# Attention in a hybrid encoder layer: query blocks run on over the heads, scores as two 64-row tiles, V turned in the projection banks

## What is computed

```
def _diff_attention(q, k, v, lam):
    # q, k: (B, 8 heads, 2 components, S, 64); v: (B, 8, S, 128)
    def block(qblk):                      # 128 queries
        s = einsum('bhcqd,bhckd->bhcqk', qblk, k) * scale
        p = softmax(s, axis=-1)
        a = p[:, :, 0] - lam * p[:, :, 1]
        return einsum('bhqk,bhke->bhqe', a, v)
    return lax.map(block, qb)
```

## Time and profile before

| | before |
|---|---|
| median of 3 runs | 1740.48 us (1738.78 to 1741.96) |
| profiled execution | 1740.36 us, span 1738.6 us |
| TensorE matmul busy | 1655.1 us, 95% |
| VectorE busy | 1037.4 us, 60% |
| ScalarE busy | 755.8 us, 43% |
| GpSimd busy | 771.0 us, 44% |
| chain that ended last | PE 60%, DVE 19%, ACT 10%, issue 10% |
| mean granted clock of TensorE | 0.990 |

### The profile page before, as it was taken

How to read it: one execution, slowest core, us unless ns; L and a number is a source line. 1 busy time by engine, 2 the same in 40 slices (tenths; PEclk the granted TensorE clock), 3 DMA queues, 4 the chain that set the end, 5 groups by cost and what they waited for, 6 DMA issues and landing times.

```text
span 1738.6 us, 24563 instructions
## 1 busy us (share of the span) xinstructions
PE 1655.1 (95%) x8235; PEld 1355.8 (78%) x8235; DVE 1037.4 (60%) x1692; ACT 755.8 (43%) x1462; POOL 771.0 (44%) x926
## 2 busy tenths in 40 slices
PE   4999999999999998999999999999999999999995
PEld 3788887887878877878787878787877788888784
DVE  6703676776676767787878787878776101235213
...
GB/s 169 13 134 30 31 49 73 24 51 70 24 60 61 25 86 61 37 61 40 57 41 55 42 54 45 52 45 51 48 61 49 254 128 259 169 74 95 121 72 97
DMA packets 137300, 129.08 MB, mean 74 GB/s; under 512 B 5089, under 2 KB 120354, under 8 KB 136226
## 3 DMA queue, kind: packets, MB, share of 16 engines
...
...
## 4 chain that ended last, share of the span: by engine, by line
PE 60%; DVE 19%; ACT 10%; issue 10%; DMA 1%; DVEq 1%; ACTq 0%; SPq 0%
PE ps L621 45%; PE ps L629 7%; DVE negmax L1351 2%; PE ps L803 2%; PE ps L811 2%; ACT probs L1794 2%; ACT aT_split L1799 2%; DVE aT_split L1356 1%; DMA v_f<-in_x 1%; DVE h_sum L1304 1%; DVE raw_b L1038 1%; DVE mix L1343 1%; DVE q_stack L1286 1%; DVE sigmoid_work L1038 1%; DVE h_sum L1234 1%
## 5 line engine op out<-in xcount | busy, mean ns | idle before, releaser
L621 PE MATMUL ps<-xn_split,w_split 128*128 128x512 f32 x4224 | 1032.9, 401 | 2.4 <-ACT v_f L1501 1.9
L621 PEld LDWEIGHTS ps<-xn_split,w_split 128*128 128x128 f32 x4224 | 789.5, 189 | 187.1 <-POOL w_split L560 2.3
L554 POOL TENSOR_TENSOR w_split<-w_raw,ones 128x256 fp32r<-128x256 f32 x416 | 318.8, 796 | 855.9 <-PE ps L621 812.8
L560 POOL TENSOR_TENSOR w_split<-w_raw,w_split 128x256 fp32r<-128x256 f32 x416 | 329.3, 822 | 8.2
L1794 ACT ACTIVATE probs<-ps,negmax 128x1024 f32<-128x1024 f32 x128 | 143.0, 1117 | 139.0 <-DVE negmax L1351 139.0
L621 PE MATMUL ps<-h_split,w_split 128*128 128x512 f32 x768 | 181.2, 396 | 0.1
L621 PEld LDWEIGHTS ps<-h_split,w_split 128*128 128x128 f32 x768 | 143.4, 188 | 35.1 <-issue 0.5
L1351 DVE TENSOR_REDUCE negmax<-ps 128x1 f32<-128x1024 f32 x128 | 150.2, 1214 | 4.5 <-PE ps L803 4.5
L1356 DVE TENSOR_TENSOR aT_split<-ps,aT_split 128x512 fp32r<-128x512 f32 x128 | 88.5, 691 | 90.5 <-ACT aT_split L1799 89.6
L803 PE MATMUL ps<-k_stack,q_stack 128*128 128x512 f32 x512 | 135.7, 407 | 7.0 <-DMA k_stack<-k_stack 7.0
L803 PEld LDWEIGHTS ps<-k_stack,q_stack 128*128 128x128 f32 x512 | 92.4, 191 | 25.7 <-DMA k_stack<-k_stack 5.4
...
## 6 DMA issues: line engine op xcount, KB each, us to landing
...
```

What stands on the lines that cost most here:

```text
L554: hi = pool.tensor_tensor(wsp[b][:, 0, ks_], raw[b][:, ks_], ones[:, 0:1].unsqueeze(2).to_broadcast([P, SPLIT_K, P]), ALU.mult)
L560: lo = pool.tensor_tensor(wsp[b][:, 1, ks_], raw[b][:, ks_], wsp[b][:, 0, ks_].bitcast(F32), ALU.subtract)
L621: mm = pe.matmul(ps[:, half, :], wsp[b][:, wl, k, :], moving[:, xl, k, cols], start=(k == 0 and n == 0), stop=(k == KT - 1 and n == 2))
```

## The change

- Scores: Q and K are stored as plain high and low parts, both components one over the other. A matmul contracts 64 rows: component 0 on rows 0 to 63, component 1 on rows 64 to 127, alternating, into different banks. Three passes by two halves by two components are twelve matmuls a block. Both components of the scores are ready together. The doubling DMAs go.
- K has two buffers, by the parity of the head. The loop over heads is unrolled by two. Scores of head h + 1, block 0, are issued in block 7 of head h, and so are its maxima, exponentials and mix. K and Q of the next head are split in blocks 5 and 6.
- The mix is two steps: the first product starts after the first exponential, ahead of the second low part. On ScalarE both high copies stand ahead of both exponentials.
- The filler: head 0 as before does one half ahead of its blocks; after that even blocks take 10 k-steps (8 in head 0) and odd blocks 6.
- V's transposes go to banks 1 and 0, in blocks 0 and 1 (head 0: ahead of the blocks and in block 0).
- ScalarE squares the output from PSUM, VectorE no longer does. The gate's clamp moves to VectorE's end of block 0, its three activations to ScalarE's end of block 0. The output's steps and the shuffles move by a block.

The diff, cut to its core (engine by engine: names, SyncE, TensorE, VectorE, ScalarE):

```diff
+def fills(first):
+    return (0, 8) + tuple(8 + 14 * (q // 2) + 8 + 6 * (q % 2) for q in range(ST)) if first else \
+        (0, 0) + tuple(16 * (q // 2) + 10 + 6 * (q % 2) for q in range(ST))
+def halves(first, q):
+    at = fills(first)
+    return [n for n in range(8) if at[q + 1] < 8 * (n + 1) <= at[q + 2]]
...
-        qs = sb("q_stack", [P, 2, S], F32R, at=a_scope)
-        ks = sb("k_stack", [P, 2, 2, S], F32R, at=a_scope)
+        qs = sb("aq_split", [P, 2, S], F32R, at=a_scope)
+        ks = [sb(f"ak_split{i}", [P, 2, S], F32R, at=a_scope) for i in range(2)]
...
-def double_keys(hh):
-    own = (slice(0, AD), slice(AD, P))
-    for c in range(2):
-        sp.wait_ge(a_qk_lo.sem, a_qk_lo.after(hh, c))
-        sp.dma_start(ks[own[1 - c], c].bitcast(F32), ks[own[c], c].bitcast(F32)).then_inc(k_doubled, 16)
...
-def a_scores(h, q):
+def a_scores(h, par, q):
     if q == 0:
-        pe.wait_ge(k_doubled, 32 * h + 32)
-        pe.wait_ge(a_qk_lo.sem, a_qk_lo.after(h, 3))
-    for c in range(2):
-        if q > 0:
-            pe.wait_ge(a_exp.sem, a_exp.after(h, 2 * (q - 1) + c))
-        elif not is_zero(h):
-            pe.wait_ge(a_exp.sem, a_exp.after(h, c) - 2)
-        for i in range(2):
-            for b in range(2):
-                mm = pe.matmul(ps[:, 2 + 2 * c + i, :], qs[:, c, q * P:(q + 1) * P],
-                               ks[:, c, b, i * HALF:(i + 1) * HALF], start=(b == 0), stop=(b == 1))
-        mm.then_inc(a_score.sem, 1)
+        pe.wait_ge(a_qk_lo.sem, a_qk_lo.after(h, 1))
+    if not (is_zero(h) and q == 0):
+        pe.wait_ge(a_exp.sem, a_exp.after(h, 2 * q - 1))
+    for i in range(2):
+        for n, (a, b) in enumerate(PASSES):
+            for c in range(2):
+                rows = slice(c * AD, (c + 1) * AD)
+                mm = pe.matmul(ps[:, 2 + 2 * c + i, :], qs[rows, a, q * P:(q + 1) * P],
+                               ks[par][rows, b, i * HALF:(i + 1) * HALF], start=(n == 0), stop=(n == 2))
+                if i == 1 and n == 2:
+                    mm.then_inc(a_score.sem, 1)
+def mix_round(h, q, i):
+    if i == 0:
+        pe.wait_ge(a_mix.sem, a_mix.after(h, 5 * q + 4))
+    if not (is_zero(h) and q == 0 and i == 0):
+        pe.wait_ge(a_tr_read.sem, a_tr_read.after(h, 2 * q + i - 1))
+    for n in range(4):
+        k = 4 * i + n
+        mm = pe.transpose(ps[:, 6, n * P:(n + 1) * P], am[q % 2][:, k * P:(k + 1) * P], ident[:])
     mm.then_inc(a_tr.sem, 1)
+def v_round(h, i, tile_half):
+    pe.wait_ge(proj_read, tile_half)
+    for n in range(4):
+        c = 4 * i + n
+        mm = pe.transpose(ps[:, 1 - i, n * P:(n + 1) * P], vz[:, 0, c * P:(c + 1) * P], ident[:])
+    mm.then_inc(a_vtr.sem, 1)
 def pv(h, n):
-    pe.wait_ge(a_tr_read.sem, a_tr_read.after(h, round_of(2 * n + 1, 1)))
-    if n > 0:
-        pe.wait_ge(a_rs.sem, a_rs.after(h, 2 * (n - 1)))
-    elif not is_zero(h):
-        pe.wait_ge(a_rs.sem, a_rs.after(h, 0) - 2)
+    pe.wait_ge(a_tr_read.sem, a_tr_read.after(h, 4 * n + 3))
+    if n == 0:
+        pe.wait_ge(a_vlo.sem, a_vlo.after(h, 1))
+    if not (is_zero(h) and n == 0):
+        pe.wait_ge(a_of.sem, a_of.after(h, 2 * n - 1))
     for k in range(KT):
         mm = product(ps[:, 7, 0:2 * P], lambda a: va[:, a, k, :], lambda b: at_s[:, b, k, :],
                      start=(k == 0), stop=(k == KT - 1))
...
 def squares(h, n):
-    pe.wait_ge(a_osq.sem, a_osq.after(h, n))
+    pe.wait_ge(a_of.sem, a_of.after(h, 2 * n + 1))
+    if not (is_zero(h) and n == 0):
+        pe.wait_ge(a_rs.sem, a_rs.after(h, 2 * (n - 1)))
     pe.matmul(ps[:, 7, 2 * P:4 * P], ones[:], osq[:], start=True, stop=True).then_inc(a_ss.sem, 1)
-def a_head(h, first, last):
...
-    a_scores(h, 0)
+def a_head(h, par, first, last):
+    at = fills(first)
+    base, per_head, hh = (G_GL, 0, 0) if last else (G_A, 4, h)
+    def filler(begin, end):
+        for n in range(8):
+            lo, hi = max(begin, 8 * n), min(end, 8 * n + 8)
+            if lo < hi:
+                if lo == 8 * n and n in (1, 2):
+                    pe.wait_ge(a_vlo.sem, a_vlo.after(h, n - 1))
+                proj_half(base, per_head, hh, n // 2, n % 2, begin=lo - 8 * n, end=hi - 8 * n)
+    read_by = 2 * (G_A + 4 * h)
     if first:
-        pe.wait_ge(proj_read, 2 * (G_M + 8 * (MH - 1) + 7) + 2)
-    v_round(0)
-    filler(0)
-    if not first:
-        squares(h - 1, 3)
+        a_scores(h, par, 0)
+        v_round(h, 0, read_by)
+        filler(0, at[1])
     for q in range(ST):
         mix_round(h, q, 0)
         if q + 1 < ST:
-            a_scores(h, q + 1)
-        else:
-            filler(7, begin=4, end=6)
+            a_scores(h, par, q + 1)
+        elif not last:
+            a_scores(h + 1, 1 - par, 0)
         mix_round(h, q, 1)
+        if q == 0 and not first:
+            v_round(h, 0, read_by)
+            squares(h - 1, 3)
+        if q == (0 if first else 1):
+            v_round(h, 1, read_by + 1)
         if q % 2 == 0 and q > 0:
             squares(h, q // 2 - 1)
-        if q < 5:
-            filler(q + 1, amid=(lambda: v_round(1)) if q == 0 else None)
-        elif q == 5:
-            filler(6, end=4)
-        elif q == 6:
-            filler(6, begin=4)
-            filler(7, end=4)
-        else:
-            filler(7, begin=6)
+        filler(at[q + 1], at[q + 2])
         if q % 2 == 1:
             pv(h, q // 2)
...
+def k_low(hh, par):
+    dve.wait_ge(a_qk_hi.sem, a_qk_hi.after(hh, 0))
+    dve.tensor_tensor(ks[par][:, 1], qkf[:, 1], ks[par][:, 0].bitcast(F32), ALU.subtract) \
+        .then_inc(a_qk_lo.sem, 1)
+def q_low(hh):
+    dve.wait_ge(a_qk_hi.sem, a_qk_hi.after(hh, 1))
+    dve.tensor_tensor(qs[:, 1], qkf[:, 0], qs[:, 0].bitcast(F32), ALU.subtract).then_inc(a_qk_lo.sem, 1)
...
+def mix_first(h, q):
+    b = q % 2
+    dve.wait_ge(a_exp.sem, a_exp.after(h, 2 * q))
+    dve.reciprocal(rden[:, 0, 0:1], den[:, b, 0:1]).then_inc(a_mix.sem, 1)
+    dve.wait_ge(a_mix.sem, a_mix.after(h, 5 * q))
+    dve.tensor_scalar(am[b][:], pr[:, 0], rden[:, 0, 0:1], None, ALU.mult).then_inc(a_mix.sem, 1)
+def mix_second(h, q):
+    b = q % 2
+    dve.wait_ge(a_exp.sem, a_exp.after(h, 2 * q + 1))
+    dve.reciprocal(rden[:, 0, 1:2], den[:, b, 1:2]).then_inc(a_mix.sem, 1)
+    dve.wait_ge(a_mix.sem, a_mix.after(h, 5 * q + 2))
+    dve.tensor_scalar(rden[:, 1, 0:1], rden[:, 0, 1:2], neglam[:], None, ALU.mult).then_inc(a_mix.sem, 1)
+    dve.wait_ge(a_mix.sem, a_mix.after(h, 5 * q + 3))
+    dve.scalar_tensor_tensor(am[b][:], pr[:, 1], rden[:, 1, 0:1], am[b][:], ALU.mult,
+                             ALU.add).then_inc(a_mix.sem, 1)
...
+def a_head(h, par, first, last):
+    if first:
+        maxima(h, 0)
+        mix_first(h, 0)
+        v_low_round(h, 0)
+        mix_second(h, 0)
     for q in range(ST):
+        a_low_round(h, q, 0)
+        nxt = (h, q + 1) if q + 1 < ST else None if last else (h + 1, 0)
+        if nxt is not None:
+            maxima(*nxt)
+            mix_first(*nxt)
+        a_low_round(h, q, 1)
+        if q == 0 and not first:
+            v_low_round(h, 0)
+        if q == (0 if first else 1):
+            v_low_round(h, 1)
+        if nxt is not None:
+            mix_second(*nxt)
         if q == 0:
+            dve.wait_ge(proj_read, 2 * (4 * h + G_A))
+            dve.tensor_scalar(aw[:], vz[:, 1], -1.0, LARGEST, ALU.mult, ALU.min).then_inc(a_gate_dve.sem, 1)
         if q == 1:
             if not first:
+                o_out_gate(h - 1, 3)
+                dve.wait_ge(a_ost.sem, a_ost.after(h - 1, 7))
             dve.wait_ge(a_gate_act.sem, a_gate_act.after(h, 2))
             dve.scalar_tensor_tensor(ga[:], vz[:, 1], again[:], aw[:], ALU.mult, ALU.mult) \
                 .then_inc(a_gate_dve.sem, 1)
+            if not first:
+                o_out_low(h - 1, 3)
+        if q in (2, 4) and not last:
+            shuffle(h + 1, q - 2)
+        if q in (3, 5, 7):
+            o_out_gate(h, q // 2 - 1)
+            o_out_low(h, q // 2 - 1)
+        if q == 5 and not last:
+            k_low(h + 1, 1 - par)
+        if q == 6 and not last:
+            q_low(h + 1)
...
+def exps(h, q):
     b = q % 2
+    for c in range(2):
+        if not (is_zero(h) and q == 0):
+            act.wait_ge(a_mix.sem, a_mix.after(h, 5 * q - 1))
         act.wait_ge(a_max.sem, a_max.after(h, 2 * q + c))
         act.activation(pr[:, c], ps[:, 2 + 2 * c:4 + 2 * c, :].rearrange("p b k -> p (b k)"), ACT.Exp,
                        bias=nmax[:, b, c:c + 1], accum_out=den[:, b, c:c + 1]).then_inc(a_exp.sem, 1)
+def v_high_round(h, i):
+    if i == 0 and not is_zero(h):
+        act.wait_ge(a_pv.sem, a_pv.after(h, -1))
+    act.wait_ge(a_vtr.sem, a_vtr.after(h, i))
+    act.activation(va[:, 0, 4 * i:4 * i + 4, :], ps[:, 1 - i, :].rearrange("p (k s) -> p k s", k=4),
+                   ACT.Copy).then_inc(a_vhi.sem, 1)
 def o_read(h, n):
     act.wait_ge(a_pv.sem, a_pv.after(h, n))
+    if not (is_zero(h) and n == 0):
         act.wait_ge(a_ost.sem, a_ost.after(h, 2 * (n - 1)))
```

(31 more changed lines are left out.)

226 lines of the change are left out of this document (53 added, 173 removed).

## The result

The changed kernel took 1751.61 us (median, 1749.46 to 1754.4), the kernel before 1740.03 beside it: ratio 1.0066, 95% interval 1.0048 to 1.0085. It is 11.6 us slower where 18 us less were forecast, and outside the forecast's range. The profiled execution took 1754.4, its span 1752.6. Two single executions that took far longer than the rest of theirs (8366.3 of the kernel before, beside the later runs, and 2028.2 of all_three) are left out of the ratios.

A forecast was written before the change was run, and what follows sets the result against it. TensorE was taken as the bound, but not alone: busy 582.16 of 603.96 us over seven heads. The last product ending 19.4 earlier, less 1.5 for the clock, gave 17.9 off 1740.36: 1722.4 us, range 1705 to 1748.

The forecast's parts named there:

- pair slot: Scores: two 64-row matmuls on both array halves run together in 0.237 us, so six pairs take 1.42.
- x: Time from a block's first four transposes to its second four; 2.05 forecast in q3, more where low parts come late.
- T: Moment when a block's first four transposes start on TensorE; other times in the block count from it, in us.
- dear switches: Rival: entering or leaving 64-row tiles costs 0.4 us, not 0.1; 17 lost in all, 1739, no change; chance 0.08.
- The start: Attention's opening: first scores at 656.0, first transposes of head 0 at 664.1 against 670.37 before.
- q0: First of a head's eight blocks, q0 to q7; forecast 10.5 us, second transposes 2.32 after the first.
- Block by block: Step walking through a steady head's eight blocks: sum 84.3 us a head against 86.28, 2.0 gained.
- q1: Block 1 of a head: new wait behind the gate's clamp and activations, 2.6 us long; block forecast at 13.0.
- the clock falls in every head: Rival: TensorE's clock drops behind the block 1 wait in seven more heads, 1.5 us each; 1733; chance 0.12.
- work alone would have given: Per head: 7.5 us gain from work alone, beside the 2.0 forecast.
- serial pairs: Rival: score pairs do not overlap, twelve matmuls take 2.84 us; 52 lost in all, 1774; chance 0.17.
- longer queues in front of the single bank: Case: the 5.5 us of waits walked through turn out a third longer; 1737, no chance of its own.

The follow-up runs named there:

- all_three: Apparently the changed kernel with output steps moved, gate earlier and output read behind the high copy, 1700.89 us; the study never ties this name to a run.
- moved: Changed kernel with the output's steps on VectorE and ScalarE put behind the mix of the even blocks; 1716.94 us, ratio 0.9867.

## Why the prediction was wrong

*Right.* The pair slot: twelve 64-row matmuls take 1.65, and with both switches x = 2.12 in a quiet block; T + 2.0 to 2.3 was forecast. The switches are cheap (rival "dear switches": it needed x = 2.58), though going in costs 0.17 and not 0.1: the scores start at T + 0.53, before at T + 0.36. The start within 0.3. No wait on the mix. Head 7 took 83.2 (83.2): the clock fell there behind a wait of 1.89, but cost nothing, since block 1 and block 2 together take 23.7 with the fall and 23.6 in the kernels where it held, as the wait of 1.4 in block 2 goes with it.

*Luck.* Head 0 took 80.1 (78.4, or 79.9 with the 1.5 put down for the clock): the clock did not fall in this execution, and blocks 4, 5 and 6 were longer by about as much. Block q0 took the 10.5 of the forecast with an x 0.2 shorter and the work behind it 0.2 longer.

*The step that failed* is "Block by block": the six heads took 538.1 (from 744.42 to 1282.56) against 505.8, 32.3 more, and the five lines q2 to q6 hold 30.7 of it. The miss has three parts, in the order of size.

First, the durations of VectorE's steps. The forecast placed each moved step by its length in the earlier trace rows: 0.2 + 0.2 + 1.29 for the mix, some 1.3 for K's low part. In the new order they lie beside other steps of GpSimd, and take 1.03 instead of 0.75, 1.42 instead of 1.29, 1.72 instead of 1.3. The terms it missed are 0.5 in q2, 0.8 in q3, 0.6 in q4, 0.8 in q5 and 1.1 of q6's 2.4, so 3.8 a head, 22.9 in all. In q2, q4 and q6, 0.15 each of this is TensorE's own: from the second transposes to the next T a block with 10 k-steps takes 7.91, in moved too, where 7.76 was counted. That is 2.7 of the 22.9. In q3 and q5, a product now waits up to 0.44 for a low part that stands behind a mix product of 1.86. GpSimd's rope was costed in the forecast only for when it ends, not for whom it holds up. Proof: cut it and the splits, and the heads come in at or below the forecast's time. As q2 and q6 were placed later than the steps' own lengths put them, by 0.8 and 0.9, the delays beside GpSimd are dearer than the miss shows. Put the steps elsewhere, and 37 of the stage's 706.8 go with no work removed.

Second, the clock. The forecast looked for it in q1, behind a wait of 2.6. That wait measured 1.76 in the steady heads and left the clock alone; in head 0 it was 3.33, and this execution kept its clock there, as did three others, while seven lost 1.5 to 2.7 in that block (14.67 to 15.85 against 13.13). The chain there was over-sized: the clamp began at T0 + 8.74 instead of 9.3, so the copy started at T1 + 2.58 instead of 3.3, 0.83 a head that came back (5.0). The fall came in q6, where the wait was 2.15 instead of 1.4: five heads, 1.6 each, 7.9. The rival "the clock falls in every head" had the price right, 1.5 a head, and the place wrong: it put the fall in q1.

Third, the jump of the loop. It was not in the forecast at all: two waits of 1.8 and 1.7, and once slow scores behind it, 5.4 in the profiled execution. That the body of TensorE's loop doubled was in the diff.

22.9 + 7.9 + 5.4 - 5.0 = 31.2 of the 32.3; the rest are 0.1 a block in q7 and a slip in the forecast's sum, whose eight blocks add up to 84.4 and not 84.3. Another number there, the 7.5 that "work alone would have given", is not worked out: by its own terms it would be 86.28 - (80.4 - 8 x 0.31) = 8.4. Nothing of the forecast rests on it. The rival on the slower side was the wrong one: serial pairs (17 in 100), while longer queues in front of the single bank had no chance of their own and a price of only 1737.

*What stays open.* Why ScalarE's step starts 0.08 later in the loop than written out is not shown: the trace has only the start. Why the clock did not fall in head 1's block 6, at a wait as long as in the others, nor in head 0 in four executions of eleven, was not tried. Nor was how many matmuls the two row halves take ahead beyond three.
